# A streaming encoder layer on one core: the FFN up product by one Strassen level, its features through DRAM, and the down product in three rounds

## What is computed

```python
u, g = jnp.split(jnp.einsum('btd,df->btf', h, w_up), 2, axis=-1)
u_ext = jnp.concatenate([conv_past.astype(u.dtype), u], axis=1)
c = conv_b + u_ext[:, 0:t] * conv_w[0]
for i in range(1, CONV_W):
    c = c + u_ext[:, i:i + t] * conv_w[i]
y = jax.nn.gelu(c, approximate=True) * g
return jnp.einsum('btf,fd->btd', y, w_down), u_ext[:, -(CONV_W - 1):]
```

## Time and profile before

| what | value |
|---|---|
| median of 3 runs | 1637.05 us (1634.82 to 1637.43) |
| profiled execution, span from first to last instruction | 1636.5 us |
| its own time around that span | not given apart; the runs shown lie 1.7 below to 0.9 above the span |
| TensorE busy | 1577.5 us, 96% |
| TensorE weight loads busy | 1473.6 us |
| DVE, ACT, POOL busy | 963.8, 439.8, 556.4 us |
| from the first to the last FFN matmul | 858.3 to 1624.5 us |
| DMA | 123.16 MB, mean 75 GB/s |

### The profile page before, as it was taken

How to read it: one execution, slowest core, us unless ns; L and a number is a source line. 1 busy time by engine, 2 the same in 40 slices (tenths; PEclk the granted TensorE clock), 3 DMA queues, 4 the chain that set the end, 5 groups by cost and what they waited for, 6 DMA issues and landing times.

```text
span 1636.5 us, 24360 instructions
## 1 busy us (share of the span) xinstructions
PE 1577.5 (96%) x9351; PEld 1473.6 (90%) x9351; DVE 963.8 (59%) x1836; ACT 439.8 (27%) x920; POOL 556.4 (34%) x304
## 2 busy tenths in 40 slices
PE   6999999999999999999999999999999999999997
PEld 5899999999989988897879989999898998989995
DVE  6876667767752488764545554554544545445456
ACT  5143534344342255563321101011010110101013
POOL 5522222222222322252323334434344342534342
PEclk9999999999999999999999999999999999999998
DMA  6222222121134411175321112111021111111115
GB/s 188 80 69 75 84 91 75 45 81 49 35 126 162 165 29 55 53 255 172 129 68 30 52 30 61 49 42 51 26 64 38 51 38 38 51 46 43 51 51 107
DMA packets 129918, 123.16 MB, mean 75 GB/s; under 512 B 8517, under 2 KB 116425, under 8 KB 129841
## 3 DMA queue, kind: packets, MB, share of 16 engines
q1 hardware_dynamic: 93945, 67.17, 14.0%
q10 hardware_dynamic: 34840, 51.14, 9.3%
q0 software_dynamic: 1056, 3.80, 1.3%
HBM read 95.84 MB, written 27.93 MB: 76 GB/s over the span
## 4 chain that ended last, share of the span: by engine, by line
PE 83%; DVE 9%; ACT 2%; DMA 2%; issue 2%; POOL 1%; ACTq 1%; SPq 0%; DVEq 0%; POOLq 0%
PE bank L751 17%; PE bank L752 17%; PE bank L753 17%; PE bank L757 7%; PE bank L759 7%; PE bank L758 7%; PE bank L783 4%; PE bank L892 2%; PE bank L863 1%; PE bank L862 1%; DVE rowsn L1738 1%; DVE kl L1759 1%; DMA raw<-in_w_o 1%; PE bank L1143 1%; PE bank L1144 1%
## 5 line engine op out<-in xcount | busy, mean ns | idle before, releaser
L633 POOL TENSOR_TENSOR ring_h<-raw,att 128x1024 fp32r<-128x1024 f32 x107 | 207.4, 1939 | 917.7 <-PE bank L753 745.9
L751 PE MATMUL bank<-m_h,ring_h 128*128 128x352 f32 x1056 | 340.7, 323 | 0.7 <-DVE m_l L1645 0.7
L752 PE MATMUL bank<-m_l,ring_h 128*128 128x352 f32 x1056 | 338.6, 321 | 0.0
L753 PE MATMUL bank<-m_h,ring_l 128*128 128x352 f32 x1056 | 338.4, 320 | 0.0
L634 POOL TENSOR_TENSOR ring_l<-raw,ring_h 128x1024 fp32r<-128x1024 f32 x107 | 285.7, 2670 | 8.4
L751 PE MATMUL bank<-ht_h,ring_h 128*128 128x352 f32 x816 | 269.2, 330 | 2.0 <-POOL ring_l L634 1.3
L753 PE MATMUL bank<-ht_h,ring_l 128*128 128x352 f32 x816 | 263.4, 323 | 0.0
L752 PE MATMUL bank<-ht_l,ring_h 128*128 128x352 f32 x816 | 262.9, 322 | 0.0
L751 PEld LDWEIGHTS bank<-m_h,ring_h 128*128 128x128 f32 x1056 | 198.1, 188 | 1.2 <-DVE m_l L1645 0.8
L752 PEld LDWEIGHTS bank<-m_l,ring_h 128*128 128x128 f32 x1056 | 198.4, 188 | 0.3
L753 PEld LDWEIGHTS bank<-m_h,ring_l 128*128 128x128 f32 x1056 | 198.0, 188 | 0.0
(11 more groups left out here) (294 smaller groups left out, 2610.9 us busy)
## 6 DMA issues: line engine op xcount, KB each, us to landing
raw<-in_w_up SPq DMA_DIRECT2D x44, 512.0 KB, 3.8
raw<-in_w_in SPq DMA_DIRECT2D x34, 512.0 KB, 3.8
raw<-in_w_down SPq DMA_DIRECT2D x22, 512.0 KB, 3.6
d_gate<-gst ACTq DMA_DIRECT2D x48, 176.0 KB, 1.9
gm<-d_gate ACTq DMA_DIRECT2D x8, 528.0 KB, 4.4
d_mfox<-mst ACTq DMA_DIRECT2D x8, 528.0 KB, 2.9
gate<-d_gate ACTq DMA_DIRECT2D x24, 176.0 KB, 3.1
fox<-d_mfox ACTq DMA_DIRECT2D x24, 176.0 KB, 4.1
```

The source lines that it names most:

```text
L633: order.link(nc.gpsimd.tensor_tensor(high, src, zero.to_broadcast(list(src.shape)), ALU.add))
L751: nc.tensor.matmul(out, wh, xh, start=start, stop=False)
L752: nc.tensor.matmul(out, wh, xl, start=False, stop=False)
L753: return nc.tensor.matmul(out, wl, xh, start=False, stop=stop)
```

## The change

It alters the FFN alone.

*Tokens* are cut into two halves of 528 (`HB`), each in two chunks of 264 (`CB`). *Features 0 to 2* (`PLAIN` = 3) are computed as before, but in eight chunks of 264 with a bank each, all evicted by ACT: 192 matmuls of 264 columns per feature. *Features 3 to 21* use one level of a Strassen scheme in Winograd's form. The 2 x 2 blocks of the product are: model dimensions in two halves of 512 (4 k tiles), outputs u and v, tokens in two halves. Seven products P1 to P7 of half depth replace eight: 7 x 2 chunks x 4 k tiles x 3 = 168 matmuls of 264 columns. They run in the order P1, P6, P2, P7, P5, P4, P3; P2, P7, P4 and P3 accumulate onto a bank that already holds P1, P6, P7 and P5.

New elementwise work for it:
- once, during the plain features, seven adds or subtracts of [128, 4 x 528] on DVE (`first_tokens`, `last_tokens`) and three on POOL (`token_sum`); the four sums are split into high (ACT, `token_high`) and low (DVE, `token_low`);
- per split feature, four sums of weight blocks on POOL (`weight_sums`, 512 columns each), seven highs on ACT (`weight_high`) and seven lows on POOL (`weight_lows`);
- per split feature, ten evictions with an add on DVE (`u_sum`, `out_sum`, 264 columns) and four copies on ACT.

u and v both go to SBUF; the convolution, gelu and gate work on whole tiles of 1058 columns, and the result is stored to DRAM (`d_y`, `y_store`, 528 KB a feature).

*The down product* comes after the whole up product, in three rounds of three token tiles (`ROUNDS`); six banks accumulate over all 22 features, so nothing is added in SBUF. A step is one feature of one round (66 steps): its y columns are loaded (`y_load`), split by ACT and DVE (`y_high`, `y_low`), and w_down's slab, now loaded once per round, is split by ACT and POOL (`down_high`, `wd_l`) into 8 slots (`NW`); y has 6 (`NY`). The matmuls are 1144 of 512 columns again: 16 in a step of round 0, 18 in the others. In the last round the three tiles run one step behind each other. Finished tiles are squared, scaled and stored between steps (`FINALS`).

Core of the diff, with the parts that the prediction speaks of:

```diff
+HB = TOK // 2
+CB = HB // 2
+PLAIN = 3
+PRODUCTS = ["P1", "P6", "P2", "P7", "P5", "P4", "P3"]
+ROUNDS = [[NT, 0, 1], [2, 3, 4], [5, 6, 7]]
+NW, NY = 8, 6
...
# SP
+            def up_load(f, j):
...
+                else:
+                    sp.wait_ge(w_ready, blocks_made(f - 1, ("P2", "P4")[j]))
+                sp.dma_start(raw[:, n % NRAW], cols(wup, j * FF + f * P)).then_inc(raw_in[n % NRAW], 16)
+            def down_load(j):
...
+                    sp.wait_ge(wd_ready, j - NRAW + 1)
...
+            for j in range(4):
+                y_load(j)
+            for j in range(2, 4):
+                down_load(j)
+            y_store(FT - 1)
+            for j in range(4, N_STEPS):
+                y_load(j)
+                down_load(j)
...
# POOL
+            for f in range(1, PLAIN):
+                plain_slabs(f)
+                if f == 1:
+                    pool.wait_ge(t_free, T_MIX + HALVES)
+                    pool.wait_ge(up_full, 1)
+                    token_sum()
...
+            for f in range(PLAIN, FT):
+                weight_sums(f)
+                weight_lows(f)
...
# TensorE
+            def half_product(f, name, c, b, xh, xl, fresh_bank):
+                pe.wait_ge(w_ready, blocks_made(f, name))
+                wh, wl = slot(name)
+                for k in range(4):
+                    mm = three(bank[b][:, 0:CB], wh[:, k, :], wl[:, k, :], xh[:, k, CB * c:CB * c + CB],
+                               xl[:, k, CB * c:CB * c + CB], fresh_bank and k == 0, k == 3, not fresh_bank)
+                mm.then_inc(up_full, 1)
...
+                    if f == 0:
+                        if i == 5:
+                            mix_transposes(NT)
...
+                        elif i >= 8:
+                            pe.wait_ge(down_free, i - 7)
...
# ScalarE, plain features
+                    plain_evict(f, i)
...
+                    if f == 1 and i == 1:
+                        token_high(2)
+                    if f == 1 and i == 3:
+                        gelu(0)
+                    if f == 1 and i == 5:
+                        token_high(0)
+                    if f == 2 and i == 1:
+                        token_high(3)
+                    if f == 2 and i == 3:
+                        gelu(1)
+                    if f == PLAIN - 1 and i == 4:
+                        weight_high(PLAIN, "P1")
...
# VectorE
+            first_tokens()
+            last_tokens()
+            conv_taps(0, (0, 1, 2))
+            token_low(2)
+            token_low(0)
+            gated(0)
...
+            for f in range(PLAIN, FT):
+                conv_taps(f - 1, (0, 1))
+                u_sum(f, "u2", 0)
+                u_sum(f, "u2", 1)
+                conv_taps(f - 1, (2,))
...
+                gated(f - 1)
+                out_sum(f, "c21", 0)
...
+            for j in range(4):
+                y_low(j)
+            conv_taps(FT - 1, (0, 1, 2))
+            gated(FT - 1)
...
+            for j in range(4, N_STEPS):
+                y_low(j)
...
+                if j in (FT + 3, 2 * FT + 3):
+                    r = j // FT - 1
...
+                    for n in range(3 * r, 3 * r + 3):
+                        down_out(n)
```

More of the change, by code:

```diff
@@ L229, in program @@
     assert o2 + 4 * D <= R3
[L231 to L239, removed]
+    tb = []
@@ L600, in _ @@
[L600 to L610, removed]
+            def up_load(f, j):
+                n = S_FFN + 2 * f + j
+                if f == 0:
+                    sp.wait_ge(slab_split, n - NRAW + 1)
+                elif f - 1 < PLAIN:
+                    sp.wait_ge(slab_split, n - NRAW + 1)
+                else:
+                    sp.wait_ge(w_ready, blocks_made(f - 1, ("P2", "P4")[j]))
+                sp.dma_start(raw[:, n % NRAW], cols(wup, j * FF + f * P)).then_inc(raw_in[n % NRAW], 16)
@@ new lines, in _ @@
+            up_load(0, 0)
+            up_load(0, 1)
+            up_load(1, 0)
+            up_load(1, 1)
+            for f in range(FT):
+                for j in range(2):
+                    if f + 2 < FT:
+                        up_load(f + 2, j)
+                    elif f + 2 == FT:
+                        down_load(j)
+                    if j == 0 and f >= 1:
+                        y_store(f - 1)
+            for j in range(4):
+                y_load(j)
+            for j in range(2, 4):
+                down_load(j)
@@ new lines, in _ @@
+            y_store(FT - 1)
+            for j in range(4, N_STEPS):
+                y_load(j)
+                down_load(j)
+                if j == 10:
+                    sp.wait_ge(up_full, UP_ALL)
+                    sp.dma_start(g_fin[:, :], norm_ffn_post.to_broadcast([P, D])).then_inc(fin_in, 16)
+                    for s in range(2):
+                        sp.wait_ge(x1_out[s], 16 * (5 - s))
+                    sp.dma_start(xlast[:, :], tok_rows(y_prompt[0], y_sample[0], NT - 1)).then_inc(x_last, 16)
@@ new lines, in _ @@
+            for r in range(len(ROUNDS)):
+                last = r == len(ROUNDS) - 1
+                for q in range(FT + (LAG if last else 0)):
+                    if r == 0 and q == 8:
+                        pe.wait_ge(conv_done, FT)
+                        pe.wait_ge(up_dve, dve_evicted(FT - 1, "c12", 1))
+                        for k in range(4):
+                            mm = nc.tensor.transpose(bank[5][0:FT, P * k:P * k + P], tails[:, k, :], ident)
+                        mm.then_inc(misc_pe, 1)
+                    for pos in range(3):
+                        k = q - (pos if last else 0)
+                        if not 0 <= k < FT:
+                            continue
+                        j = FT * r + k
+                        if pos == 0:
+                            pe.wait_ge(wd_ready, j + 1)
+                            pe.wait_ge(yt_ready, j + 1)
+                        for e in range(2):
+                            mm = down_tile(j, pos, e, 3 * r + pos)
+                            if k == FT - 1:
+                                mm.then_inc(down_full, 1)
+                            elif pos == 2 and e == 1:
+                                mm.then_inc(down_read, 1)
@@ L1599, in _, with gelu, u_free @@
-            act.wait_ge(down_free, 4)
-            ffn_features(0, 0, True)
-            with act.Fori(0, (GROUPS - 1) // 2) as m:
-                g = m * 2 + 1
-                ffn_features(g, 1)
-                ffn_features(g + 1, 0)
-            for n, t in enumerate(DOWN[:NT]):
+            def gelu(f):
+                act.wait_ge(conv_done, f + 1)
+                nc.scalar.activation(conv[f % 2][:, :], conv[f % 2][:, :], ACT.Gelu_apprx_tanh).then_inc(gelu_done, 1)
+            def u_free(f):
+                wait(act, conv_done, f - 1)
@@ new lines, in _ @@
+            for f in range(PLAIN, FT):
+                more = f + 1 < FT
+                p1_out(f, 0)
+                p1_out(f, 1)
+                if f == PLAIN:
+                    token_high(1)
+                if more:
+                    weight_high(f + 1, "P1")
+                    weight_high(f + 1, "P6")
+                c11_out(f, 0)
+                c11_out(f, 1)
+                if more:
+                    weight_high(f + 1, "P2")
+                gelu(f - 1)
+                if more:
+                    for name in PRODUCTS[3:]:
+                        weight_high(f + 1, name)
```

678 lines of the change are left out of this document (475 added, 203 removed).

## The result

The changed kernel takes 1670.02 us (median of 4 runs, 1669.6 to 1671.11) and the kernel before 1637.24 beside it: a ratio of 1.0202, 95% interval 1.0188 to 1.0216. It is slower by 32.8 us where 13 us less were forecast. The profiled execution has a span of 1669.2 us (before 1636.5) at a mean granted clock of 0.976.

What follows compares the result with a forecast made beforehand. The prediction took TensorE's matmul columns to bound the FFN: -45.5 us for columns, less the gains lost to waits, supply and clock, and -2 for the tail, summed to -13.3, giving 1624 us; own range 1610 to 1638.

Steps and rivals of the forecast that it cites:

- rounds 1 and 2 stay TensorE's: Down product, later rounds: w_down supply at 3.87 us a step keeps up with 4.08 us of matmuls, adding nothing.
- round 2: Last round of the down product: +1 us at its start, a lead of about a step having grown.
- Rival B: Down product: raw buffers bound it at 4.6 us a step, POOL's low holding the next load; 1669 us, chance 0.17.
- plain features, two waits: Features 0 to 2: TensorE waits for u of f=2, +9.8 us, and for the weights of f=3, +2.6.
- rival C: Split features: the v load loop through POOL and DVE adds 1 us a feature, +19; 1643 us, chance 0.10.
- up to down: Start of the down product: step 0 waits for DVE's low of the features, behind the last eviction, +1.5 us.
- step 4: Down product, round 0: slab 4 comes late because the last features' store stands ahead of its loads, +6.3 us.
- supply in round 0: Down product, round 0: slabs come every 3.87 us against 3.63 of matmuls, 17 x 0.24 = +4 us.
- step 22: First step of round 1: the second tile waits for a bank that DVE frees late, +5 us.
- slow clock behind pauses: After two long TensorE idle times, at f=2 and the fourth down step, a lower granted clock costs +4 us.
- tail: End of the kernel: six of the eight accumulating stores are long done, -2 us.
- Rival A: Whole FFN: weights and tokens arrive in time, so the stalls are covered; 1594 us, chance 0.17.

Runs made afterwards that it cites:

- exact counts: Changed kernel with three waits on down_read (features' load, both high copies) corrected for the round-end steps that do not raise it: 1624.12 us, ratio 0.9921.
- the four edits: Changed kernel with exact counts, last features' store behind step 7's loads, POOL's token sum behind the third plain slice's split, PSUM copies two steps earlier: 1607.45 us.
- the half cure: Changed kernel with each waited-for count above 22 lowered by one, except where it is 44: 1634.95 us, ratio 0.9992.

## Why the prediction was wrong, and where it was right

**The step that failed** is "rounds 1 and 2 stay TensorE's", with "+1" for the boundary of round 2. The forecast bounds the supply by the turn of the raw buffers alone, 3.87 us a step against 4.08, and has no term for the features' load: that it waits for down_read, that the weight's load stands behind it on SyncE, and that the counter isn't raised at every step. Round 2 cost 139.3 us for 89.8. With exact counts it costs 90 (the 401 matmuls of the row above in 91.0 us), and the kernel 1624.1 against a forecast of 1624. That match is partly luck, since the other terms were off in both directions.

**Rival B's time was 1669** and the result 1670, but B is false. It decides where the raw buffers are the tight loop; SyncE's 18 waits in round 2 name TensorE, POOL idles 6.9 us in the beat, and with exact counts the same buffers carry a slab in 4.1 us without a wait of TensorE's. In the stretch 1360 to 1430 SyncE does wait for POOL, 19 times and 46.8 us in all, as B has it, and TensorE has no wait there but that of step 22. A time that fits is no evidence for its mechanism.

Term by term, from the profile of the changed kernel:

| step of the forecast | forecast us | measured us |
|---|---|---|
| one matmul of 264 columns | 0.1216 | 388.54 / 3191 = 0.1218 |
| plain features, two waits | +9.8 and +2.6 | 7.1 and 1.7, in the places named |
| split features (rival C: +19) | 0 | 0.3, TensorE busy 388.1 of 389.0 |
| up to down | +1.5 | 3.7 |
| step 4 | +6.3 | 6.8 |
| supply in round 0 | +4 | 1 at most |
| step 22 | +5 | 4.1 |
| round 2 | +1 | +49.5, its slow clock included |
| slow clock behind pauses | +4 | 8.5 outside round 2 (up to 17 in it) |
| tail | -2 | -2.0 (10.4 for 12.4) |

The rows, with -44.8 for the columns, add to 35.9 us, and the profiled spans differ by 32.7. The first up matmul starts 1.5 us earlier than before (856.83 for 858.29); the rest isn't explained.

- **Columns.** The interpolation between rows 3 and 5 was right to 0.2%, and the pace is the same with exact counts and with the four edits.
- **The weights of f = 3.** I put this wait on ACT, whose first high of f = 3 was to come at t = 83 behind gelu(1). It came at 930.17, which is t = 73, and POOL made the wait: it sat idle for the second slab, whose load stood behind the store of f = 0 on SyncE (issued at 925.36). The size was luck.

```profile
930.47 1.82 POOL L878 TENSOR_TENSOR sw<-raw 128x512 f32<-128x512 f32 x1 [12.72 <-DMA raw<-in_w_up]
```

- **Up to down.** I counted the low half of the features only; TensorE waited for POOL's low half of the first w_down slab, 2.2 us more.
- **Supply.** The 18 steps from step 4 on take 68.6 us (1354.25 to 1422.86) for 65.3 of matmuls, and 2.3 of the rest is slow clock. The page gives a landing of 3.7 us, not my 3.9; by my own formula that is +2.5, and even less shows. The gaps of the w_o rows were too wide a model.
- **Clock.** I priced two pauses. There were four outside round 2 and nine in it.
- **Rival A** is false: five waits show. **Rival C** is false: behind the first weights of f = 3 the split features have one wait, 0.34 us for a low of DVE's.

## What to carry to other kernels

A number in a wait says how far ahead it lets go only if every step raises the counter: find the steps that raise another one instead, and count in the last round as well as in the first. Where the same wait comes back every n steps and the engine named was idle before it, walk the chain back to the event that released it and compare its length to the lead: here a lead of three steps gave no wait, one of two steps a few, and one of one step a stall in every beat. And look one queue further before moving work away from a wait: the sum and the loads that were moved here came back as waits elsewhere, the store as two small ones, and the count and the copies did not. Before a stall is put down to a count, look whether its transfer landed in the usual time: one of the two long waits of the half cure was a slab that took 7.9 us.

## What the runs showed of the hardware

**The long waits cost twice.** After the waits of 3.3 to 7.1 us TensorE is granted half its clock, the 1.2 GHz level, for 7 to 13 matmuls of 512 columns: they start 0.427 us apart instead of 0.227. After some waits, that of step 0 and those of round 2, the first one to three matmuls still go at full pace. The changed kernel's stretches right behind the waits of u of f = 2, of step 4 and of step 22:

```profile
911.65:915.65 4.00, 4.00 (x19) 4.00 (x20) 3.93 (x3) 0.00 (x0) 3.92 (x2) 0.54 0.47 135
...
1354.25:1359.01 4.76, 4.76 (x12) 3.39 (x12) 2.70 (x3) 1.76 (x6) 2.44 (x2) 0.50 0.69 194
...
1428.47:1434.18 5.71, 5.71 (x14) 4.45 (x15) 3.63 (x6) 2.23 (x3) 4.50 (x2) 0.50 0.25 86
```

In the last, 13 matmuls take 5.71 us for 2.95, which makes 2.8 us; the waits of round 2 cost 1.7 each on top of themselves. Behind waits of 1.7 us and less the clock stays: the changed kernel behind 1.67 us, and the kernel with the later store behind 0.99:

```profile
938.53:941.00 2.47, 2.47 (x20) 2.47 (x21) 2.19 (x2) 2.47 (x7) 2.47 (x3) 1.00 0.00 0
```

```profile
1374.53:1377.50 2.97, 2.97 (x13) 2.30 (x14) 2.97 (x3) 0.09 (x1) 2.60 (x1) 1.00 0.60 189
```

Between the two the length of the wait doesn't settle it. In the kept traces every wait of 2.9 us or more from the up product on is followed by the lower level and none of 1.73 or less is, but of those between, some are: in the kernel with the later store the one of 1.79 us (first row), and in the kernel with the weight's load first the one of 2.21 us (second row), where the one of 2.76 us isn't (third row):

```profile
937.30:940.30 3.00, 3.00 (x16) 3.00 (x17) 2.68 (x3) 2.62 (x7) 3.00 (x3) 0.62 0.00 0
...
1554.55:1558.00 3.45, 3.45 (x10) 2.80 (x11) 0.56 (x1) 1.47 (x2) 0.67 (x1) 0.65 0.51 154
...
1591.21:1594.20 2.99, 2.99 (x13) 2.50 (x14) 0.56 (x1) 1.09 (x2) 2.58 (x2) 1.00 0.67 110
```

So a wait of about 4 us costs 5.4 to 6.9 in all by these rows, and one of 1.5 costs the 1.5.

**Small instructions pay for the shared port too.** The same DVE copy of two columns takes 0.16 us with POOL at rest and 4.65 beside POOL's sum, which ends with it, at 906.9:

```profile
902.27 4.65 DVE L2556 COPY uext<-cwt 128x2 f32<-128x2 f32 x1
...
924.86 0.16 DVE L2556 COPY uext<-cwt 128x2 f32<-128x2 f32 x1
```

The Trainium skill (GPSIMD Engine Reference, Specifications) says that POOL's SBUF interface is shared with VectorE, with contention where a DVE instruction reads two SBUF inputs or runs in a two-port mode. The sums, which read two SBUF inputs, agree with it; the copy reads one, and no trace shows its mode. The rows show how the interface is shared: a whole instruction at a time, so that the short one waits for the long one to end.
